# Five token runs of 1, 1, 2, 2 and 3 tiles instead of three, and ranking one group ahead of its dots

## The reference

```python
h = rmsnorm(x)
z = h @ w_in                       # 1024 x 2720: latents, rotary key, diff q/k/v, memory q
o_a = latent attention(z, w_uq, w_uk, w_uv);  o_b = differential attention(z)
o_m = attention into 256 memory tokens
g_a, g_b, g_m = split(sigmoid(h @ w_gate + b_gate))          # w_gate 1024 x 3072
x = x + (g_a*(o_a @ w_br_a) + g_b*(o_b @ w_br_b) + g_m*(o_m @ w_br_m)) @ w_o
t = rmsnorm(x)
q = t @ peer_wq                    # 1024 x 2048: 8 heads x 2 halves
s1, s2 = top16(q[:, 0] . subkeys), top16(q[:, 1] . subkeys)
best, idx = top16 of the 256 sums s1 + s2;   g = softmax(best)
a = gelu(peer_u[idx] . t)
x = x + sum(g * a * peer_v[idx])   # 8 heads x 16 experts a token
y = rmsnorm(x)
```

## Time and profile before

| | us |
|---|---|
| median of 3 runs | 4415.14 |
| lowest and highest | 4411.97, 4420.18 |
| profiled execution | 4452.41 |
| its span, first to last instruction | 4450.6 |
| PE, DVE, ACT, POOL busy | 2849.2, 2446.5, 795.1, 2346.7 |
| moved by DMA | 1388.83 MB, 312 GB/s on average |

### The profile page before, as it was taken

How to read it: one execution, slowest core, us unless ns; L and a number is a source line. 1 busy time by engine, 2 the same in 40 slices (tenths; PEclk the granted TensorE clock), 3 DMA queues, 4 the chain that set the end, 5 groups by cost and what they waited for, 6 DMA issues and landing times.

```text
span 4450.6 us, 39027 instructions
## 1 busy us (share of the span) xinstructions
PE 2849.2 (64%) x12071; PEld 1499.1 (34%) x12071; DVE 2446.5 (55%) x6358; ACT 795.1 (18%) x1696; POOL 2346.7 (53%) x2128
## 2 busy tenths in 40 slices
PE   7779668777897878677777799783233233233334
PEld 5468546434453434443434344341000000000000
DVE  1241454677344456387788455566665666666651
ACT  1230012333111112133333111111000000000000
POOL 0000224344343346376666564567777777777774
PEclk9769889777998989877777899896555555656556
DMA  7244668777977979899999998899999999999998
GB/s 243 89 140 137 227 233 309 252 257 263 330 274 267 341 274 397 284 331 355 339 337 330 362 373 322 319 376 363 363 375 366 379 371 378 368 370 364 371 367 284
DMA packets 552141, 1388.83 MB, mean 312 GB/s; under 512 B 51296, under 2 KB 253024, under 8 KB 551936
## 3 DMA queue, kind: packets, MB, share of 16 engines
q0 software_dynamic: 304128, 1107.43, 67.0%
q1 hardware_dynamic: 227408, 249.27, 17.1%
q10 hardware_dynamic: 20400, 29.64, 2.0%
HBM read 1326.10 MB, written 60.05 MB: 311 GB/s over the span
## 4 chain that ended last, share of the span: by engine, by line
PE 34%; POOL 23%; issue 13%; DVE 12%; DMA 10%; ACT 4%; DVEq 2%; another core or an unknown queue 1%; SPq 1%; ACTq 0%; POOLq 0%
POOL G_v_rows L569 12%; POOL G_u_rows L569 11%; PE scores L695 8%; PE scores L1452 8%; PE y_sum L1942 4%; PE scores L1456 4%; PE scores L1641 3%; DVE G_u_rows L1778 3%; DMA G_v_rows<-in_peer_v,G_idxT 2%; PE scores L1538 2%; DMA DF_w_br<-scratch_skT 2%; ACT C_probs L1260 2%; DVE C_probs L1327 1%; PE o L1209 1%; DVE C_probs L1351 1%
## 5 line engine op out<-in xcount | busy, mean ns | idle before, releaser
L569 POOL DMA_INDIRECT G_v_rows<-in_peer_v,G_idxT x1056 | 1180.9, 1118 | 1066.6 <-PE y_sum L1942 720.9
L1778 DVE CUSTOM_DVE_ANT_0 G_u_rows<-G_u_rows,G_h 128x1024 f32<-128x1024 f32 x1056 | 1276.3, 1221 | 529.5 <-DMA G_u_rows<-in_peer_u,G_idx 482.5
L569 POOL DMA_INDIRECT G_u_rows<-in_peer_u,G_idx x1056 | 1161.6, 1100 | 726.7 <-issue 314.4
L1942 PE MATMUL y_sum<-G_v_rows,G_zw 128*32 128x512 f32 x4224 | 792.5, 888 | 1000.9 <-DMA G_v_rows<-in_peer_v,G_idxT 961.8
L1942 PEld LDWEIGHTS y_sum<-G_v_rows,G_zw 128*32 128x32 f32 x4224 | 155.7, 142 | 1531.5 <-issue 1526.2
L1452 PE MATMUL scores<-D_hT,D_w_gate 128*128 128x256 f32 (+2 forms) x768 | 238.2, 464 | 0.0
L695 PE MATMUL scores<-A_w_in,A_hT 128*128 128x256 f32 (+2 forms) x864 | 223.5, 420 | 9.7 <-ACT A_hT L783 5.6
L695 PEld LDWEIGHTS scores<-A_w_in,A_hT 128*128 128x128 f32 x864 | 171.1, 200 | 63.3 <-issue 14.3
L1192 PE MATMUL turn<-ident,C_probs 128*128 128x128 f32 (+1 forms) x647 | 142.1, 337 | 72.1 <-ACT C_pT L1272 52.5
L1452 PEld LDWEIGHTS scores<-D_hT,D_w_gate 128*128 128x128 f32 x768 | 145.2, 191 | 92.7 <-issue 54.2
L548 POOL MEMSET G_zw<- 128x1024 f32 x2 | 1.8, 956 | 292.8 <-SPq L521 292.8
(11 more groups left out here) (282 smaller groups left out, 3822.0 us busy)
## 6 DMA issues: line engine op xcount, KB each, us to landing
A_w_in<-in_w_in SPq DMA_DIRECT2D x24, 1024.0 KB
D_w_gate<-in_w_gate SPq DMA_DIRECT2D x24, 1024.0 KB
G_u_rows<-in_peer_u,G_idx POOLq DMA_INDIRECT x1056
G_v_rows<-in_peer_v,G_idxT POOLq DMA_INDIRECT x1056
DF_w<-in_w_gate SPq DMA_DIRECT2D x12, 1024.0 KB
DF_w<-in_peer_wq SPq DMA_DIRECT2D x12, 1024.0 KB
F_w_q<-in_peer_wq SPq DMA_DIRECT2D x12, 1024.0 KB
G_sc<-scratch_sc ACTq DMA_DIRECT2D x66, 128.0 KB
```

The costliest lines, as they stand in the source:

```text
L569: pool.indirect_dma_start(out=buf[:, :], out_offset=None, in_=table, in_offset=bass.IndirectOffsetOnAxis(ap=rows, axis=0)).then_inc(signal ...
L1778: dve.tensor_tensor_reduce(out=self.u_rows[slot][:, :], in0=self.u_rows[slot][:, :], in1=self.h2[t % 2][:, :], scale=1.0, scalar=0.0, op0= ...
L1942: last = pe.matmul(self.ps_y[32 * c:32 * (c + 1), cols], self.zw[b % 2][:, at:at + 32], self.v_rows[(4 * quad + c) % SLOTS_G][:, cols], st ...
```

## The change

`SPANS` has five entries, for tiles 0, 1, 2-3, 4-5 and 6-8. `AHEAD` is 1: the pieces of the ranking of group n + 1 stand after dots 0, 2, 4 and 6 of group n, its gate after dot 8 instead of 15, ACT's exponential at step 5 instead of 10. The plan follows: run 0 ends with step 21, the others must end 24 steps ahead of their first tile's first dot instead of 48, that is with 105, 233, 489 and 745. The rest lets runs have one tile.

```diff
--- before.py
+++ after.py
@@ -68,7 +68,7 @@
         self.cols = slice(self.lo, self.lo + self.width)
 
 
-SPANS = [Span(i, lo, hi) for i, (lo, hi) in enumerate(((0, 2), (2, 5), (5, TILES)))]
+SPANS = [Span(i, lo, hi) for i, (lo, hi) in enumerate(((0, 1), (1, 2), (2, 4), (4, 6), (6, TILES)))]
 STAGES = [(sp.i, name) for sp in SPANS for name in ("inputs", "memory", "attend", "merge", "out", "score")
           if name != "memory" or sp.i == 0]
 AT = {stage: i for i, stage in enumerate(STAGES)}
@@ -185,7 +185,7 @@
 BLOCK = 2 * TOPK
 V_LAG = 48
 STEPS = U_SLOTS + V_LAG + 4
-AHEAD = 2
+AHEAD = 1
 QUADS = BLOCK // 4
 
 
@@ -310,7 +310,7 @@
         m["v_diff"] = sb(ctx, f"C_v_diff{i}", [P, vt, P])
         m["q_mem"] = sb(ctx, f"C_q_mem{i}", [P, sp.width])
         m["k_mem"], m["v_mem"] = sb(ctx, f"C_k_mem{i}", [P, 2, MEM]), sb(ctx, f"C_v_mem{i}", [P, 2, 2, P])
-        top = sp.keys
+        top = max(sp.keys, MEM)
         m["probs"] = [sb(ctx, f"C_probs{i}_{k}", [P, top]) for k in range(6)]
         m["pT"] = [sb(ctx, f"C_pT{i}_{k}", [P, max(top, 2 * P)]) for k in range(2)]
         m["o"] = {k: sb(ctx, f"C_o_{k}{i}", [P, nt, P]) for k in ("mla", "diff", "mem")}
@@ -477,10 +477,10 @@
             own = [(name, cost) for i, name, cost in ticks if i == sp.i]
             if sp.i == 0:
                 out += [0] * (len(own) - 2 * HEADS)
-                out += [0] * 5 + [1, 2] + [2 + 3 * k for k in range(1, 2 * HEADS - 6)]
+                out += [0] * 5 + [1] + [1 + 2 * k for k in range(1, 2 * HEADS - 5)]
                 done = out[-1]
                 continue
-            end = 2 + P * sp.tiles[0] - (AHEAD + 1) * TOPK
+            end = AHEAD + P * sp.tiles[0] - 24
             total, sofar = sum(cost for _, cost in own), 0.0
             for _, cost in own:
                 sofar += cost
@@ -499,7 +499,7 @@
         assert tick == len(plan), (tick, len(plan))
         for _ in steps:
             done += 1
-        assert done == STEPS + 2, done
+        assert done == STEPS + AHEAD, done
 
     def dense(self, inputs, memory, attend, merge, out, score, eng):
         for sp in SPANS:
@@ -587,7 +587,8 @@
 
         self.load_x(eng, sp, 0)
         eng.dma_start(self.A[sp.i]["g_mix"][:, :], self.a["norm_mix"].to_broadcast([P, D])).then_inc(self.a_g, 16)
-        self.load_x(eng, sp, 1)
+        if sp.nt > 1:
+            self.load_x(eng, sp, 1)
         self.load_w_in(eng, sp, 0)
         self.load_w_in(eng, sp, 1)
 
@@ -1407,6 +1408,8 @@
                 maximum(j + 2)
             yield
         take_o(len(jobs) - 1)
+        if o.last["diff"] + 2 == o.n:
+            norm_o(PAIRS - 1)
         dve.drain().then_inc(self.dve_left, 1)
 
 
@@ -1519,7 +1522,7 @@
             yield
         store(nt - 1)
         self.load_score(eng, sp, 0)
-        for k in range(2):
+        for k in range(min(2, nt)):
             eng.wait_ge(self.e_out[k], self.e_out0[k][i] + 32 * ((nt + 1 - k) // 2))
 
     def out_pe(self, pe, sp):
@@ -1784,9 +1787,9 @@
                 self.weigh(dve, n - 1)
             m = n + AHEAD
             if m < GROUPS_ALL:
-                if c in (3, 6, 9, 12):
-                    self.rank(dve, m, c // 3 - 1)
-                if c == 15:
+                if c in (0, 2, 4, 6):
+                    self.rank(dve, m, c // 2)
+                if c == 8:
                     self.gate(dve, m)
             if k in finish:
                 self.finish_sum(dve, finish[k])
@@ -1881,12 +1884,9 @@
         act.wait_ge(self.made, 9)
         act.dma_start(self.g_fin[:, :], self.a["norm_final"].to_broadcast([P, D])).then_inc(self.g_fin_in, 16)
         self.load_scores(act, 0)
+        self.load_h2(act, 0)
         self.load_scores(act, 1)
-        self.load_h2(act, 0)
         self.gate_exp(act, 0)
-        self.load_scores(act, 2)
-        yield
-        self.gate_exp(act, 1)
         yield
         finish = {tile_end(t) + 2: t for t in range(TILES)}
         for k in range(STEPS):
@@ -1896,12 +1896,12 @@
                 act.activation(self.gelus[(n - 1) % 2][:, :], self.dots[(n - 1) % 2][:, :], ACT.Gelu).then_inc(self.gelu_done, 1)
             if c == 2 and n % 2 == 0 and 2 <= n <= GROUPS_ALL:
                 self.spread(act, n // 2 - 1)
-            if c == 8 and n + 3 < GROUPS_ALL:
-                self.load_scores(act, n + 3)
-            if c == 10 and n + AHEAD < GROUPS_ALL:
+            if c == 8 and n + AHEAD + 1 < GROUPS_ALL:
+                self.load_scores(act, n + AHEAD + 1)
+            if c == 5 and n + AHEAD < GROUPS_ALL:
                 self.gate_exp(act, n + AHEAD)
             t = n // HEADS
-            if n % HEADS == 4 and c == 5 and t + 1 < TILES:
+            if n % HEADS == 6 and c == 12 and t + 1 < TILES:
                 self.load_h2(act, t + 1)
             if n % HEADS == 6 and c == 5 and t < KEY_TILES:
                 self.load_x1(act, t)
@@ -1966,7 +1966,7 @@
 
         @block.sync
         def _(sp):
-            k.weave(k.dense(k.inputs_sp, k.memory_sp, k.attend_sp, k.merge_sp, k.out_sp, k.score_sp, sp), idle(sp, STEPS + 2))
+            k.weave(k.dense(k.inputs_sp, k.memory_sp, k.attend_sp, k.merge_sp, k.out_sp, k.score_sp, sp), idle(sp, STEPS + AHEAD))
 
         @block.tensor
         def _(pe):
```

## The result

| | before, us | with the change, us |
|---|---|---|
| median (4 runs each) | 4417.66 | 4608.91 |
| lowest and highest | 4411.97, 4420.75 | 4598.87, 4616.87 |
| profiled execution | 4452.41 | 4609.73 |
| its span | 4450.6 | 4607.6 |

The ratio is 1.0433, with a 95% interval from 1.0409 to 1.0457: the change makes the kernel 4.3% slower. Forecast were 4556 us, with a range of 4380 to 4690.

A forecast was written before the change was run, and what follows sets the result against it. Data movement bounds the second half; the loss stands at the front. Run 0 405, runs 1 to 4 470, 675, 1000, 1050, rest 993: 4593, +1.8 = 4595, scaled by 4415.14 / 4452.41 to 4556 us; range 4380 to 4690.

The forecast's parts named there:

- run 0: First dense stretch, tile 0 alone: inputs and attention 205 us, merge 75, output projection 25, scores 100, in sum 405.
- run 1: Second dense stretch, tile 1, 84 steps: D 423, P 263, plus 47 us for short stages awaiting first weights, 470.
- run 2: Third dense stretch, tiles 2 and 3, 128 steps: D 584, P 526, plus 91 us, 675.
- run 3: Fourth dense stretch, tiles 4 and 5, 256 steps: D 960, P 666, plus 40 us, 1000.
- run 4: Last dense stretch, tiles 6, 7 and the sample, 256 steps: D 992, P 798, plus 58 us, 1050.
- rest: After run 4, gathers alone: 312 dots at 2.871 us, 896, plus the tail of 97, 993 us.
- rival (b): TensorE's narrow matmuls wait for weights and get clock 0.5: +160 us in all, 4755, on the median's scale 4715; chance 0.14.
- D: A later run's DMA load: steps times 2.871 us plus megabytes of SP loads and oT stores by 0.327 per us.
- P: A later run's PE load: 960 weight-stationary matmuls, the tiles' own work and 0.62 us a step for y matmuls.
- Rival (a): Dense runs: longer overlap fills the DMA and seams shrink; 4416 us with a quarter of them, 4322 with none; chance 0.20.
- Rival (c): Bunched ranking delays dots where DVE has dense work too: 2 us in each of 47 groups, +94, 4650; chance 0.05.
- Rival (d): First run's scores wait for their loads, so no early start: first gather near 445, +100, 4655 us; chance 0.02.

## Why the prediction was right, point by point

| | forecast, us | measured, us |
|---|---|---|
| first u gather | 345 | 352.8 |
| run 0 | 405 | 402 |
| run 1 | 470 | 488 |
| run 2 | 675 | 691 |
| run 3 | 1000 | 963 |
| run 4 | 1050 | 1074 |
| rest | 993 | 990 |
| sum of the profiled execution | 4595 | 4609.7 |
| median | 4556 | 4608.9 |

**The early start** is as forecast, run 0 in part by luck: inputs and attention took 217 us (205 forecast), the merge 74 (75), the output projection 29 (25) and the scores 81 (100), so the errors cancel. The narrow matmul cost what the neighbours at 64 and 256 columns said. (All such prices, and the counts of 576 and 960, are by record, two for each matmul.) In the changed run 0's merge (timeline of PE), sixteen records of 128 columns start at 255.21 and the next group at 257.00, so 0.112 each, where 0.11 was taken:

```profile
255.21 1.95 PE L1455 MATMUL scores<-D_hT,D_w_gate 128*128 128x128 f32 x16
257.00 1.06 PE L1459 MATMUL scores<-D_oT,D_w_br 128*128 128x128 f32 x8
...
217.00:291.00 74.00, 67.03 (x576) 66.49 (x576) 11.21 (x39) 10.10 (x25) 1.18 (x2) 0.95 0.85 274
```

The window below them is that merge: 74 us, 75 in the forecast. Its granted clock was 0.95, so rival (b), the half clock, did not come. The 0.18 us that the prediction estimated from the Trainium skill's sustained spacing (TensorE: Matmul & The Clock Gate, Back-to-back issue gap) is not seen here for these 32-bit matmuls.

**The bytes** were 103 MB and cost nearly their full price in runs 1 and 3: 86 and 95 us for 100 us of DMA. That is what carries the result: without 98 of the 103 MB the loss is gone (4395.16 us).

**The larger load plus a seam** (a seam is what a run takes over the larger of D and P) gave the four dense runs 3195 us in all; they took 3216. The seams over D (423, 584, 960, 992) were 65, 107, 3 and 82 us against 47, 91, 40 and 58, so the single seams were off by up to 37, in both directions. That their sum, 257 for 236, came so close is luck; the seams were taken by likeness from two old runs, and no run here shows what sets their size. PE's loads, forecast 263, 526, 666 and 798, were 283, 542, 685 and 832. In run 3, D without a seam was enough; that mixed streams move more than their sum allows, as the earlier trace rows showed, is one reading of it, which no run here tests.

**The mis-sized term** is the last one, the scale. The sum against the profiled execution was 4595, 15 us under what was measured. I then multiplied by 4415.14 / 4452.41, which took 39 us off. That was the offset of one execution and not a property of the kernel: the profiled execution after stands 1 us from its median. Most of the miss of 53 us is this step.

**Rival (a), saturation,** fell: the DMA share in the changed runs 1 and 2 is 0.80 and 0.85, and the seams came to 257 us, where with 94 the change would have been as fast as before. **Rival (c)** fell too: packed at 0 to 6 the ranking costs nothing that shows. That left late it costs 91 us is another mechanism, gathers that wait for `G_idx`, and the change has none of it: behind the start its POOL never waits for `G_idx` ahead of a u gather. The sentence that no gather waits for the ranking holds only because the pieces were moved too. **Rival (d)** did not come.

**Two readings of the prediction were off**, without weight in the sum. A dot takes 1.22 us in the earlier trace rows (511.94 us for 418), not 1.15, which leaves its 18 us for seven steps as they are. And in the earlier trace rows the sixth slice of the DMA line is 6 and a few behind the sixteenth are 8, not 9.

What the forecast did not say is that the change has a good half. I gave the near ranking 0, and valued the steps that it lets into the dense runs nowhere by themselves. In three runs it is worth 42 us; in five it shows nothing clear of noise (4608.91 against 4619.8), as 31 steps in run 1 cost 65 us there, 2.1 each.

## What to carry to other kernels

Where one stream of transfers sets the end, a finer pipeline that reads its weights again pays for each pass in the time of that stream: compare the time that an earlier start gives with the bytes it adds, at the rate of the trace. Before cutting into more pieces, look for stretches in which neither load is full and move work of the bound stream into them; here 24 steps cost 39 us there and gave back 75 at the end. When a step is moved nearer to its use, check which wait it must beat, and move its pieces, not only its distance.

## What the runs showed of the hardware

Two loads that are each near full in one stretch hide each other's cuts. In run 2, 100 us of DMA alone gave 38 us, half of the matmuls alone (70 us less of busy PE) gave 8, and both together 90. In runs 1 and 3, where PE's load is further below the DMA's, the cuts added up as far as the run lengths tell: 86 and 12 alone and 104 together, 95 and 17 alone and 98 together.

And a 32-bit matmul with stationary weights gets no cheaper below 128 columns: its record took 0.216 us at 256 columns and 0.106 at 64, and 0.112 at 128 in the timeline above, at granted clocks of 1.00, 0.98 and 0.95 in the windows around them. So from 256 to 128 columns the price halves, and from there to 64 it stays. What sets this floor was not tested.
